# Samples' page work two tiles ahead of the prompt's tiles, and an output projection that ends with tokens standing

## The reference, cut to what matters

```
xn = RMSNorm(h);  h = h + [ S5(xn)*silu(z_s) ; MLA(xn)*silu(z_a) ] @ w_out;  y = RMSNorm(h)
prompt: w = softmax(q . k) over 528 keys, o = w . v, per head
sample: w = softmax(q_abs . c_past + q_pe . kpe_past), o_lat = w . c_past, o = o_lat . w_uv
c_past of a sample: 16 pages of 128 rows of 512 latent values, picked by page_table
```

## Time and profile before

| | |
|---|---|
| median of three runs | 1095.8 us |
| the profiled execution's own time | 1097.7 us |
| its span, first to last instruction | 1095.6 us |
| mean granted TensorE clock | 0.982 |
| TensorE busy, VectorE, ScalarE, GpSimd | 94%, 57%, 35%, 14% |

### The profile page before, as it was taken

How to read it: one execution, slowest core, us unless ns; L and a number is a source line. 1 busy time by engine, 2 the same in 40 slices (tenths; PEclk the granted TensorE clock), 3 DMA queues, 4 the chain that set the end, 5 groups by cost and what they waited for, 6 DMA issues and landing times.

```text
span 1095.6 us, 26948 instructions
## 1 busy us (share of the span) xinstructions
PE 1032.9 (94%) x10653; PEld 954.6 (87%) x10653; DVE 623.2 (57%) x1337; ACT 378.9 (35%) x797; POOL 157.6 (14%) x257
## 2 busy tenths in 40 slices
PE   5999999999999999999999999788988899999995
PEld 5999999999999999988899987565655479999995
DVE  4685535451585655678785436688888633234332
ACT  6621111211233312144651231544554413233233
POOL 0002410000130000010322512323434100000000
PEclk9999999999999999999999999889999999999998
DMA  9548643323363443265545756859999893322313
GB/s 259 121 132 151 162 107 97 84 63 98 100 168 104 108 133 96 68 153 174 152 142 154 232 179 213 264 156 280 287 282 292 226 321 104 110 78 77 86 29 156
DMA packets 201773, 169.80 MB, mean 155 GB/s; under 512 B 37548, under 2 KB 166055, under 8 KB 200103
## 3 DMA queue, kind: packets, MB, share of 16 engines
q1 hardware_dynamic: 178566, 119.12, 39.3%
q0 software_dynamic: 11616, 29.06, 8.9%
q10 hardware_dynamic: 11496, 20.32, 5.2%
HBM read 140.84 MB, written 25.26 MB: 152 GB/s over the span
## 4 chain that ended last, share of the span: by engine, by line
PE 78%; ACT 5%; SPq 5%; DVE 4%; issue 4%; DMA 3%; POOL 1%; ACTq 0%; DVEq 0%; POOLq 0%
PE gemm L2138 14%; PE gemm L2139 13%; PE gemm L2140 13%; PE gemm L2506 6%; PE gemm L2508 6%; PE gemm L2507 6%; PE misc L2410 2%; PE gemm L2425 2%; PE gemm L2455 2%; PE misc L2165 1%; PE gemm L2344 1%; SPq L518 1%; PE gemm L2346 1%; PE gemm L2345 1%; PE misc L2224 1%
## 5 line engine op out<-in xcount | busy, mean ns | idle before, releaser
L2138 PE MATMUL gemm<-xh,w_hi 128*128 128x260 f32 (+2 forms) x1056 | 301.8, 286 | 0.2 <-DVE ev L1392 0.2
L2139 PE MATMUL gemm<-xl,w_hi 128*128 128x260 f32 (+2 forms) x1056 | 299.9, 284 | 0.0
L2140 PE MATMUL gemm<-xh,w_lo 128*128 128x260 f32 (+2 forms) x1056 | 299.4, 284 | 0.0
L865 ACT ACTIVATE w_hi<-w_raw 128x2048 fp32r<-128x2048 f32 (+3 forms) x63 | 90.7, 1439 | 316.0 <-PE gemm L2140 278.5
L2138 PEld LDWEIGHTS gemm<-xh,w_hi 128*128 128x128 f32 x1056 | 198.7, 188 | 1.0 <-issue 0.4
L2140 PEld LDWEIGHTS gemm<-xh,w_lo 128*128 128x128 f32 x1056 | 199.2, 189 | 0.0
L2139 PEld LDWEIGHTS gemm<-xl,w_hi 128*128 128x128 f32 x1056 | 199.0, 188 | 0.0
L1324 DVE TENSOR_TENSOR w_lo<-w_raw,w_hi 128x2048 fp32r<-128x2048 f32 (+3 forms) x63 | 109.9, 1745 | 156.0 <-ACT w_hi L865 153.8
L2506 PE MATMUL gemm<-comb_hi,w_hi 128*128 128x260 f32 x512 | 147.7, 288 | 1.2 <-DVE comb_lo L2000 1.1
L2507 PE MATMUL gemm<-comb_lo,w_hi 128*128 128x260 f32 x512 | 145.4, 284 | 0.0
L2508 PE MATMUL gemm<-comb_hi,w_lo 128*128 128x260 f32 x512 | 145.4, 284 | 0.0
(11 more groups left out here) (399 smaller groups left out, 1978.2 us busy)
## 6 DMA issues: line engine op xcount, KB each, us to landing
w_raw<-w_in SPq DMA_DIRECT2D x35, 1024.0 KB, 6.7
ckv<-cache_ckv POOLq DMA_DIRECT2D x76, 256.0 KB, 4.0
w_raw<-w_out SPq DMA_DIRECT2D x16, 1024.0 KB, 5.8
ckv<-cache_ckv SPq DMA_DIRECT2D x52, 256.0 KB, 3.6
z_d<-ev ACTq DMA_DIRECT2D x16, 260.0 KB, 2.1
w_raw<-w_glu SPq DMA_DIRECT2D x8, 512.0 KB, 4.6
yt<-x_prompt SPq DMA_DIRECT2D x4, 1024.0 KB
o_y_p<-yt SPq DMA_DIRECT2D x4, 1024.0 KB
```

Source lines behind the costliest of these rows:

```text
L865: act.activation(w_hi[:, slot, 0:width], w_raw[:, slot, 0:width], ACT.Copy).then_inc(w_hi_ready, 1)
L2138: pe.matmul(acc, a, xa, start=k == 0, stop=False)
L2139: pe.matmul(acc, a, xb, start=False, stop=False)
L2140: last = pe.matmul(acc, b, xa, start=False, stop=k == k_tiles - 1)
```

## The change

1. `LEAD = 2`: in step `n` VectorE transposes group `n + 3` instead of `n + 1`, TensorE scores pair `(n + 2) // 2`, and all work of a complete sample `s` (maximum, exponential, spread, weights, weigh, copy, store) goes two steps earlier, from steps with `n % 4 == 0` to steps with `n % 4 == 2`. The last sample is done within step 31 and nothing of it is left after the loop.
2. Pair 0 is transposed between value products 5 and 6 into its own buffer `ct_first` (which lies over the second weight slot) and scored by TensorE behind value product 8. For this the query of sample 0 is built earlier, and the value products use a ring of three banks instead of four.
3. The page buffers are laid out anew: the sync queue loads group 5 and GpSimd groups 3 and 4. `exponential(0)`, the load of the values and a copy of rotary rows wait for the first page scores.
4. The ending: blocks 14 and 15 are computed with weights standing for tokens 256 to 511 and the samples only (264 columns), and finished first. Then for token tiles 0 and 1 the tokens stand in the array and the 256 columns of both blocks move, so the result comes out by tokens and needs neither copy nor transposes. Each of the two tiles is finished by itself and stored in two halves.

```
-        BY_SYNC = 3
+        BY_SYNC, LEAD = 5, 2
 def freed_at(i):
-            return 4 * (i // 4) + 4 + ((0, 2, 3, 4) if i // 4 < N_SAMPLE - 2 else (0, 2, 2, 2))[i % 4]
+            last = i // 4 - (N_SAMPLE - 2)
+            return 4 * (i // 4) + 4 - LEAD + ((0, 2, 3, 4) if last < 0 else (0, 2, 2, 2) if last == 0 else (0, 1, 1, 1))[i % 4]
...
 VectorE, attention
             for n in range(N_TILES):
-                if n % 4 == 0 and n:
-                    sample_max(n // 4 - 1)
+                group = n + 1 + LEAD
+                if (n + LEAD) % 4 == 0:
+                    sample_max((n + LEAD) // 4 - 1)
...
                 if n + 1 < N_TILES:
                     maximum(n + 1)
-                    turn_pages(n + 1, 0, 2)
-                if n % 4 == 0 and n:
-                    turn_sample_weights(n // 4 - 1)
+                if group < N_GROUPS_OF_PAGES:
+                    turn_pages(group, 0, 2)
+                if (n + LEAD) % 4 == 0:
+                    turn_sample_weights((n + LEAD) // 4 - 1)
...
 TensorE, attention
                 if n % 4 == 0 and n:
                     turn_last_weights(n - 1)
                     weigh_values(n // 4 - 1)
-                    spread_page_weights(n // 4 - 1)
-                if n % 2:
-                    page_scores(n // 2, 0, 6)
+                if (n + LEAD) % 4 == 0:
+                    spread_page_weights((n + LEAD) // 4 - 1)
+                pair = (n + LEAD) // 2 if n % 2 else N_PAIRS
+                if pair < N_PAIRS:
+                    page_scores(pair, 0, 6)
                 turn_weights(n)
...
             weigh_values(N_HEADS - 1)
-            spread_page_weights(N_SAMPLE - 1)
-            for c in range(4):
-                weigh_pages(N_SAMPLE - 1, c)
...
 TensorE, value products
+                    if v == 8:
+                        page_scores(0, 0, 16)
...
 TensorE, ending
+            def out_rows(t, k_tiles):
+                acc = gemm[2 * t + 1][:, 0:2 * P].rearrange("p (s n) -> p s n", s=2)
+                c = slice(N_META + t * P, N_META + (t + 1) * P)
+                for k in k_tiles:
+                    a, b = w_hi[:, :, k * P:(k + 1) * P], w_lo[:, :, k * P:(k + 1) * P]
+                    pe.matmul(acc, comb_hi[:, k, c], a, start=k == 0, stop=False)
+                    pe.matmul(acc, comb_hi[:, k, c], b, start=False, stop=False)
+                    last = pe.matmul(acc, comb_lo[:, k, c], a, start=False, stop=k == KD - 1)
+                return last
...
+            out_rows(0, range(0, 2))
+            out_turn_late(14, 0, READ + 1)
+            out_rows(0, range(2, 5))
+            out_turn_late(15, 1, READ + 2)
+            out_rows(0, range(5, KD)).then_inc(gemm_done, 1)
+            out_rows(1, range(KD)).then_inc(gemm_done, 1)
```

More of the change, by code:

```diff
@@ L1070, in head_hi, with build_query @@
                 act.activation(hh[h % 2][:], hraw[:], ACT.Copy).then_inc(head_hi_done, 1)
+            def build_query(s):
+                if s >= 2:
+                    act.wait_ge(sc_ready, 2 * s - 2)
+                for a in range(4):
+                    rows, cols = slice(32 * a, 32 * a + 32), slice(a * N_HEADS, (a + 1) * N_HEADS)
+                    act.activation(qx[rows, s % 2, :, cols], rep[rows, 0:16, :, s], ACT.Copy)
+                    last = act.activation(qxr[rows, s % 2, :, cols], rep[rows, 16:18, :, s], ACT.Copy)
+                last.then_inc(query_built, 1)
             for v in range(10):
@@ L1890, in _ @@
             maximum(0)
+            dve.wait_ge(sc_ready, 1)
             dve.wait_ge(c_t_ready, 6)
@@ L2328, in scores, with page_scores @@
                 last.then_inc(scores_ready, 1)
+            def page_scores(pair, first, last):
+                s, half = divmod(pair, 2)
+                if first == 0:
+                    pe.wait_ge(page_turned, 2 * pair + 2)
+                if first == 0 and half == 0:
+                    pe.wait_ge(query_built, s + 1)
+                    if s >= 2:
+                        pe.wait_ge(sexp_done, s - 1)
+                buffers = buffers_of(pair)
+                c0 = (s % 2) * P + half * 64
+                for r in range(first, last):
+                    for j in range(4):
+                        pe.matmul(SC[32 * j:32 * j + 32, c0:c0 + 64].rearrange("p (g t) -> p g t", g=2), qx[:, s % 2, r, :],
+                                  turned(pair)[:, buffers, j, r * 32:(r + 1) * 32], start=r == 0, stop=False)
+                if last < 16:
+                    return
+                for e in range(2):
+                    for j in range(4):
+                        last = pe.matmul(SC[32 * j:32 * j + 32, c0:c0 + 64].rearrange("p (g t) -> p g t", g=2), qxr[:, s % 2, e, :],
+                                         kt[:, buffers, j, e * 32:(e + 1) * 32], start=False, stop=e == 1)
+                last.then_inc(sc_ready, 1)
             pe.wait_ge(gemm_read, B_V + 2)
@@ L2462, in _ @@
                     scores(n + 1)
-                for i in range(N_GROUPS_OF_PAGES - 4):
+                for i in range(N_GROUPS_OF_PAGES):
                     if freed_at(i) == n and i % 4:
```

268 lines of the change are left out of this document (129 added, 139 removed).

## The result

The changed kernel takes **1107.9 us** (median of 12 runs, 1100.98 to 1115.24), the kernel before 1096.7 (12 runs): a ratio of 1.0099, 95% interval 1.0079 to 1.0120, so 11 us slower. The forecast was 1094.4 with a range up to 1104. The profiled execution of after took 1100.98 us, span 1099.1, and is the fastest of its 12; the medians carry the size of the loss, the profile its place.

What follows compares the result with a forecast made beforehand. TensorE, busy 94% of the span, was taken to bound the kernel with its work and pauses. Attention +4.2 us and ending -5.6 gave -1.4: 1096.3 against the profiled 1097.7, 1094.4 us in terms of the runs, range 1083 to 1104.

Steps and rivals of the forecast that it cites:

- The new wait: Steps n % 4 == 2: TensorE waits 2.2 us ahead of the spread for VectorE's transposed sample weights, at least 1.5.
- The pause before the values: Head's end: with copy_o moved away, TensorE's wait for copy_last_turned shrinks from 0.65 to 0.3 us a head.
- The waits for exponentials: Head's end: TensorE's waits for ScalarE's exponentials and scaled weights, 0.65 us a head, should go.
- "issue" pauses: Loop: TensorE pauses waiting for no engine's work, 0.7 us a head; a bit over half swallowed, 0.25 left.
- rival 2: Loop: the clock falls in the new pause, some 2.2 us a fall; four of eight 1103, all eight 1112; chance 0.2.
- +2.5 and -4.0: Start: step 4 begins later, +2.5 us; one pair, one spread and one weighing already done, -4.0 us of work left.
- 4.2 for six heads: Loop: a head has 2.7 us of pause instead of 2.0, +0.7 each, +4.2 us for six whole heads.
- The loop's end: Last values to output projection: gate and w_lo stand bare; with the other pauses there, +1.5 us.
- The ending: After the last matmul: less finishing work, one tile left to store, end at 1090.0; -5.6 us, bounds -4 and -6.5.
- Rival 1: Loop: the lead pays in full since VectorE isn't late; -8.7 in place of +4.2, 1081.5 us; chance 0.15.
- rival 3: Ending doesn't gain: stores in short rows run slower or standing tokens cost TensorE time; 1099 to 1105 us; chance 0.1.
- rival 4: Loop: the lead isn't reached, since pages land late; 1098 us; chance 0.05.

Runs made afterwards that it cites:

- start_and_ending: The changed kernel with LEAD = 0, so pair 0 ahead of the loop and the new ending stay: 1087.8 us (0.9921), again 1086.7 us (0.9907).
- filler: The changed kernel with ten useless 128x128 matmuls on TensorE ahead of each wait for the spread's transposed weights: 1099.6 us, ratio 1.0012 to the kernel before.
- start_only: The kernel before with the change's start alone (pair 0 among the value products, three banks, new page layout), old ending: 1091.3 us, ratio 0.9956.
- tail: The changed kernel with groups 1 to 3 of the last sample weighed behind the last values: 1103.8 us, ratio 1.0058 to the kernel before.
- lead_only: The changed kernel with the old ending, so parts 1 to 3 alone: 1109.6 us, ratio 1.0116 to the kernel before.
- ending_only: The kernel before with part 4 alone, the new ending: 1093.3 us (0.9971), again 1090.7 us (0.9958).
- lead_one: The changed kernel with a lead of one step instead of two and a sample's end at the head's end again: 1116.5 us, ratio 1.0186 to before.
- short_chain: The changed kernel without the samples' maximum on VectorE, constants in its place, weights not the reference's: 1099.2 us, ratio 1.0021 to the kernel before.
- before_pause: The kernel before with only a TensorE pause added once a head, ahead of turn_weights in steps n % 4 == 2: 1116.9 us, ratio 1.0189.

## Why the prediction was wrong

**Right: the mechanism at the head's end.** The new wait was priced at 2.2 us and is 2.4. The pause before the values was to be 0.3 and is 0.33. The waits for exponentials went, as did nearly all "issue" pauses. A clean head takes 21.2 us in the change; the shortest in start_and_ending take 19.9 to 20.2. The mean head of before is 21.1 us (147.75 / 7), that of start_and_ending too (147.96 / 7). So the bare price of the new wait is between 0.1 us a head (against the mean) and 1.0 (against the shortest), where the sum had 0.7.

**Failed: the clock was left out of the sum.** The step is rival 2, "the clock falls in the new pause", with a chance of 0.2 and the words that it decides from three falls on. By the prediction's own numbers the first does already: 1094.4 + 2.2 = 1096.6, against 1095.8 before. In the profiled execution it fell at six spreads of eight, behind four of the six pauses of the foreseen length. I weighed one row that held at 1.00 through 1.7 us against one that fell behind 2.3 as if they said "either", though the pause that I had worked out myself, 2.2 us, is nearly the one that fell. The price of a fall, 2.2 us, was right (23.3 against 21.2 in the change's heads). The Trainium skill, "TensorE: Matmul & The Clock Gate", section Part 1, has the throttled state as the default, held off by activity alone; filler agrees, since work without use held the clock at 1.00 in seven places of eight. Had the sum taken six falls, it would have said 1094.4 + 13.2 = 1107.6; that this meets the median so well is partly luck, since other terms were off as well, and the number of falls differs between executions of the same pauses (two to four in the loop's six).

**The start.** Given +2.5 and -4.0. start_only measured 5 us faster than before, so what is moved ahead of the loop is worth more than 1.5; by the timelines its first values begin at 716.04 us, those of before at 722.88. In the change that gain is gone: the first spread waits 5.4 us, the clock behind it is 0.67, and its first values begin at 722.63. The +2.5 itself was fair. By my sum the first spread stood at 716.9 (715.5 and 1.4 of VectorE); it came at 713.12 in the change, 715.78 in tail and 718.64 in lead_only, and the first values 0.3 us earlier, 3.2 and 6.0 us later than in before. The group of the sync queue was a small bound in the change, where VectorE waited 1.2 us for it and went on at 711.6, not 715.5. In tail and lead_only it waited 3.0 us; the line is lead_only's:

```profile
717.14 1.25 DVE L1797 STREAM_TRANSPOSE ct<-ckv 128x1024 f32<-128x1024 f32 x1 [2.99 <-DMA kpe<-cache_kpe]
```

So the start takes more in some executions than in the profiled one of the change, which is the fastest of its twelve.

**The loop.** From the first to the last values it was 147.75 us before and is 158.75: +11.0, where my terms (4.2 for six heads) had less than half. Five heads with a fall, at 2.1 us each, are some 10.6 of it.

**The loop's end.** From the last values to the output projection it is 5.9 us in place of 7.8. The pauses were foreseen (2.74 for `w_lo`, 1.5 before the spread and before the values), the half clock over 32 weighings (5.45 us where start_and_ending has 3.62) and a pause of 1.9 us ahead of it were not. With head 7 counted in, from 850.77 to 878.43 and from 859.14 to 887.32, it costs 0.5 us, not 1.5.

**The ending.** Given -5.6 with bounds -4 and -6.5; -5.1 in the profiles, 3 to 5 in the runs. Right in kind: the last store was issued 3.0 us behind the last matmul's end (3.2 foreseen), and 5.2 us, not 4.5, passed from there to the end. The recorded parts don't add up to the recorded times: 0.5 + 0.5 + 0.9 + 0.9 leads from 1082.3 to 1085.1 and not 1085.5, and 1.05 MB at 434 GB/s take 2.4 us and not 2.6. By its parts the forecast was 1089.1, a gain of 6.5, so the term was too large by 1.4 and the slips hid a part of that.

Rival 1 (the lead pays in full) fell with the wait; rival 3 fell with ending_only; rival 4 isn't the change's trouble in the loop, and lead_one's trace points to it. What stays open is how the 20 us of the lead divide by cause: filler gives back 9, the mean clocks allow the clock some 14 at most, and the rest is the waits and what they hide, which no single run isolates.

## What to carry to other kernels

Add up a change's pauses by length as well as by sum: the change and start_and_ending wait 18.0 and 17.2 us in the same stretch, yet one in pieces of 2.4 us and the other in pieces of at most 1.7. In that stretch the first lost its clock four times, the second not at all in one profiled execution and once in the other. When a chain of small instructions is moved to another step, look at what that step itself is short of (here both score banks at once), and at how many steps remain between a freed slot and its next use. Price a change's parts apart: here two of the three were good for 9 to 10 us, and the third took 20.

## What the runs showed of the hardware

Useless matmuls made the kernel faster: ten of 128x128 in a pause of 2.4 us, eight times, brought it from 1.0099 to 1.0012 of before, since the granted clock behind them stayed at 1.00 in seven places of eight. Without filler, behind six pauses each in the same stretch of the loop, the clock fell four, three and two times (2.4 to 2.8 us: the change, tail, lead_only), six times (2.7 to 3.5 us: before_pause) and not once (1.64 us: short_chain). It also fell once behind pauses of 1.45 and 0.70 us close together (start_and_ending, again). The length of a single pause, then, made a fall more or less likely here and didn't decide it in every case.
